# Modulation slots of the attentions, placed behind the value products of their step

## The chip, the cores and the metric

The kernel runs on one core of a Trainium2 chip. The metric is the time of one whole execution on the device, in microseconds (us). The five instruction queues of the core matter here by these names: PE is TensorE (PEld its weight loads, which overlap its products), DVE is VectorE, ACT is ScalarE, POOL is GpSimd, and SP is SyncE, which in this kernel only issues DMAs.

## What is computed

Two layers of a hybrid transformer step over 128 context tokens and 256 latent tokens, 384 tokens in three blocks of 128. Each layer modulates its input by vectors that come from a conditioning vector, mixes the tokens in three parallel branches, merges them by gates, and then runs a channel mixer (dense in layer 0, experts in layer 1). Cut to what matters:

```python
m = silu(cvec) @ w_ada[l] + b_ada[l]          # (1024,) @ (1024, 6144): the modulation
sh1, sc1, g1, sh2, sc2, g2 = split(m, 6)
h = rmsnorm(x, g) * (1 + sc1) + sh1
# mixer A, 4 heads, two maps each
p = softmax(q @ k.T * DHA ** -0.5)
oA = (p[map 0] - lam * p[map 1]) @ v          # then rmsnorm over the head
# mixer C, 8 heads on 2 key heads, a window of +-128 and a sink
oC = softmax(concat(scores, sink))[..., :-1] @ v
x = x + g1 * (sum_n sigmoid(h @ w_gate[n]) * (o[n] @ w_branch[n])) @ w_out
x = x + g2 * channel_mixer(rmsnorm(x, g') * (1 + sc2) + sh2)
```

## The kernel before

Everything is written out by hand: each engine has its own program, and semaphores are the only link between them. What stands earlier in an engine's program runs earlier on it.

**Large products.** A weight arrives in float32 in one of three buffers `raw` (slot number modulo 3). ACT copies it to `whi` (line 1571, or in two halves at line 1581), DVE computes `wlo = raw - whi` (line 2068), and PE multiplies in three passes (lines 779 to 781). SP issues the load of a slot only when the slot that had the buffer before it has been read.

**Modulation slots.** `w_ada` is not split. A slot of it is 1024 x 256 and is multiplied straight from `raw` by `ada_product` (line 796): eight products on four 32-column parts of the array, eight rows of the matrix at a time. Each slot lies in the same ring of three buffers as the other weights, and `mm_done` after it is what SP waits for before it fills that buffer again (line 522). Slots have no reader in the attention itself; their sums stay in bank 7 of PSUM and are copied out by ACT after the last of them.

**Attentions.** There are four: mixer A (kind 0) and mixer C (kind 1) in layer 0 and the same in layer 1. I call them the first to the fourth. Each has twelve steps t, a step being one head (A) or a pair of heads (C) with one block of queries; at t = 0, 3, 6, 9 the query block is that of the context and reads one block of keys, at the others it reads three. The parts of a step are:

- `scores(t)` on PE (line 1019): two products on the two halves of the array's rows, into banks 2(t%2) and 2(t%2)+1. It waits until the exponentials of t-2 have read those banks.
- `maxima(t)` on DVE (line 2250), then `exps(t)` on ACT (line 1744), then `normal(t)` on DVE (lines 2258 to 2265), which gives the weights in `ebuf`. DVE's program has `maxima(t+1)` ahead of `normal(t)`. In mixer C, DVE also adds half of a merge, `merge_sum` (line 2305), between `normal(4)` and `maxima(6)`.
- `transposes(t)` on PE (line 1037), the turn: it waits for `normal(t)`. In mixer C both maps are turned into banks 4 and 5 at every step, so it also waits for ACT's copy of the turn before it.
- `pt_copy(t)` on ACT (line 1755) takes the turned weights out of PSUM.
- `values(t)` on PE (line 1053), the value products: it waits for `pt_copy(t)`. `exps(t+2)` waits for `transposes(t)`, whose buffer it overwrites.

Ahead of the loop, scores 0 to 3 are done, and two modulation slots. In the loop PE runs, for each t: `scores(t+2)`, a modulation slot if t is in `ADA_STEPS` of this attention, `transposes(t)`, `values(t-1)`. `ADA_STEPS` is (1, 3, 5, 7, 9, 10), (1, 4, 6, 8, 10), (1, 4, 6, 9) and (1, 4, 6, 9) for the four attentions, 19 slots together. Right behind the loop PE goes on with the gate products of the next branch (lines 1110 and 1111).

Of the kernel before, what the change touches and what calls it, by code (L numbers as in the profile page):

```python
# [79 lines left out]
ADA_STEPS = {2: (1, 3, 5, 7, 9, 10), 3: (1, 4, 6, 8, 10), 4: (1, 4, 6, 9), 5: (1, 4, 6, 9)}  # L80
# [59 lines left out]
def prefix_step_kernel(nc, a, outs, const):  # L140
    y_prompt, y_sample, new_dk, new_dv, new_wk, new_wv = outs
    ctx = ExitStack()
    with ctx:
# [259 lines left out]
        def ada_slot(phase, i):  # L403

            if phase == 0:
                return FIRST_ADA[i]
            if phase == 1:
                return ADA_SLOTS[0] + 3 + RING * i
            l, kind = (phase - 2) // 2, (phase - 2) % 2
            return gate_slot(l, kind + 1, 0, 0) - ADA_SLOTS[phase] + i  # L410
# [17 lines left out]
        def ada_raw(n):  # L428

            return early[:, EARLY_BUF[n], :] if n in EARLY_BUF else raw[:, n % RING, :]  # L430
# [43 lines left out]
        def weight_col(t):  # L474

            return 1 + (T - P if t % 3 == 0 and t else 0)
# [24 lines left out]
        def raw_wait(eng, n, more=0):  # L501
            if n in EARLY_BUF:
                eng.wait_ge(side_in[EARLY_BUF[n]], early_wait(n))
            else:
                eng.wait_ge(raw_in[n % RING], more + 32 * raw_turn(n))
# [270 lines left out]
        def _(pe):  # L776
# [10 lines left out]
            def ada_product(phase, i):  # L787

                n, last, bank = ada_slot(phase, i), ADA_SLOTS[phase] - 1, 7
                if phase == 0:  # L790
                    i, last = i % 2, 1
                raw_wait(pe, n)
                w = ada_raw(n).rearrange("p (k c) -> p k c", k=KD)
                for k in range(KD):
                    j = k % 4
                    mm = pe.matmul(ps[32 * j:32 * j + 32, bank, 0:256], sil32[:, k, 30 - 2 * i:62 - 2 * i], w[:, k, :],  # L796
                                   start=(i == 0 and k < 4), stop=(i == last and k >= 4), tile_position=(0, 32 * j))
                mm.then_inc(mm_done, 1)
# [17 lines left out]
            def ada_end(phase, g=0):  # L816
                n = 2 * (GAP_SLOTS[phase] if phase in GAP_SLOTS else ADA_SLOTS[phase]) if phase else 4
                pe.wait_ge(ada_row, ada_turn(phase) if phase else g + 1)
                for c in range(2):
                    mm = pe.matmul(ps[:, 7, 256 + 32 * c:256 + 32 * c + n], adarow[:, c * P:(c + 1) * P], pick[:, 0:n],  # L820
                                   start=True, stop=True)
                mm.then_inc(ada_turned, 1)
# [185 lines left out]
            def scores(l, kind, t):  # L1008

                h, qb = t // 3, t % 3  # L1010
                if t >= 2:
                    pe.wait_ge(e_done, 24 * l + 12 * kind + t - 1)
                nk, k0 = (P, 0) if qb == 0 else (T, P)
                q, kk = (qTA, kTA[:, h, k0:k0 + nk]) if kind == 0 else (qTC, kTC[:, h // 2, k0:k0 + nk])
                for m in range(2):
                    r = slice(64 * m, 64 * m + 64)
                    c0 = score_col(t) if kind else 0
                    out, lhs = ps[:, 2 * (t % 2) + m, c0:c0 + nk], q[r, h, qb * P:(qb + 1) * P]
                    mm = pe.matmul(out, lhs, kk[r], start=True, stop=True)  # L1019
                mm.then_inc(s_done, 1)  # L1020

            def attention(l, kind):

                st0 = 24 * l + 12 * kind
                it0 = 24 * l + 12 * kind
                phase = 2 + 2 * l + kind

                def transposes(t):
                    pe.wait_ge(p_done, st0 + t + 1)
                    if kind:  # L1030
                        pe.wait_ge(pt_evac, it0 + t)
                    elif it0 + t >= 2:
                        pe.wait_ge(pt_evac, it0 + max(t - 1, 0))
                    k0 = kind * weight_col(t)
                    for m in range(1 + kind):
                        for kb in range(1 if t % 3 == 0 else 3):
                            mm = pe.transpose(ps[:, 4 + (m if kind else t % 2), kb * P:(kb + 1) * P],  # L1037
                                              ebuf[:, t % 2, m, k0 + kb * P:k0 + (kb + 1) * P], ident)
                    mm.then_inc(tp_done, 1)

                def values(t):
                    h, qb = t // 3, t % 3
                    pe.wait_ge(pt_evac, it0 + t + 1)
                    grp = 8 * l + 4 * kind + h
                    if qb == 0 and grp >= 1:
                        pe.wait_ge(o_evac, grp)
                    c = slice(h * P, (h + 1) * P) if kind == 0 else slice(512 + (h // 2) * 64, 576 + (h // 2) * 64)
                    keys = [vtok[:, 0, c]] if qb == 0 else [vtok[:, 1, c], vtok[:, 2, c], ctxv[:, c]]
                    for kb, v in enumerate(keys):
                        k = slice(kb * P, (kb + 1) * P)  # L1050
                        for m in range(1 + kind):
                            rows, x = (slice(64 * m, 64 * m + 64), ptm[:, t % 2, m, k]) if kind else (slice(0, P), pt[:, t % 2, k])
                            mm = pe.matmul(ps[rows, 6, qb * P:(qb + 1) * P], v, x, start=(kb == 0),  # L1053
                                           stop=(kb == len(keys) - 1))
                    mm.then_inc(pv_done, 1)

                scores(l, kind, 2)
                scores(l, kind, 3)
                pe.wait_ge(merge_top, 2 * l + kind + 1)
                ada_product(phase, 0)  # L1060
                ada_product(phase, 1)
                if kind == 0:
                    pe.wait_ge(merge_done, 6 * l + 2)
                else:
                    pe.wait_ge(merge_read, 4 * l + 2)
                for t in range(12):
                    if t >= 2 and t + 2 < 12:
                        scores(l, kind, t + 2)
                    if t in ADA_STEPS[phase]:
                        ada_product(phase, 2 + ADA_STEPS[phase].index(t))  # L1070
                    transposes(t)
                    if t >= 1:
                        values(t - 1)
                    if t == 11 and kind == 1:
                        ada_end(phase)
                values(11)
# [463 lines left out]
            for l in range(DEPTH):  # L1540
                if l:
                    mean_squares(2 * l)
                input_projection(l)
                branch(l, 0)
                attention(l, 0)
                branch(l, 1)
                attention(l, 1)
                branch(l, 2)
                out_projection(l)
                if l == 0:  # L1550
                    mean_squares(1)
                    units()
                else:
                    router()
                    experts()
# [1247 lines left out]
```

## Time and profile before

| | us |
|---|---|
| median of three runs | 1479.57 |
| lowest and highest of them | 1478.41, 1483.42 |
| the profiled execution | 1476.79 |
| its span in the profile | 1475.1 |
| PE busy | 1443.6 (98% of the span) |
| DVE busy | 906.6 |
| ACT busy | 729.5 |
| DMA, mean over the span | 221 GB/s |

PE is busy nearly all the time, and the granted clock is near full everywhere. The chain that ended last is PE's own work for 92% of the span. The four attentions take 25.7, 31.0, 24.7 and 30.2 us of the span. A matmul's duration in the profile overlaps the next one's, so what a piece of work costs PE is read from one start to the next start (I call this its pitch), and a wait of PE is the part of such a distance that the pitch doesn't explain.

### The profile page before, as it was taken

The numbers are of one execution on the slowest core, as the hardware profiler recorded it, in microseconds if no ns is written. First come the engines' busy times: TensorE is split into PE (matmuls) and PEld (weight loads), VectorE is DVE, ScalarE is ACT, GpSimd is POOL, SyncE is SP. The second block draws the span as 40 slices with busy tenths as digits, with TensorE's granted clock in tenths as the row PEclk, the third lists the DMA queues.
The fourth block names the chain that finished last, engine by engine and source line by source line (L and its number), as shares of the span: only waits on it lengthen the run. The fifth ranks groups of instructions, "written<-read, shape, count | busy, mean of one in ns | idle before, by whom it ended". The sixth has DMA issues, their size and how long they took to land.

```text
span 1475.1 us, 22230 instructions
## 1 busy us (share of the span) xinstructions
PE 1443.6 (98%) x8917; PEld 1273.5 (86%) x8917; DVE 906.6 (61%) x1092; ACT 729.5 (49%) x865; POOL 50.7 (3%) x55
## 2 busy tenths in 40 slices
PE   7999999999999999999999999999999999999997
PEld 5788969789999999998889879699888888888884
DVE  5543266555644345426532373747889999989888
ACT  4433354453433233225434272734568787787754
POOL 0100000000000000001000000000000000000020
PEclk9999999999999999999999999999999999999999
DMA  9854365468763355273532272655799999999991
GB/s 327 287 177 151 114 209 181 131 204 274 234 200 111 115 143 142 89 240 118 173 126 94 89 236 77 200 172 165 246 355 378 379 391 390 386 385 385 354 332 68
DMA packets 228858, 325.42 MB, mean 221 GB/s; under 512 B 8453, under 2 KB 154790, under 8 KB 228510
## 3 DMA queue, kind: packets, MB, share of 16 engines
q1 hardware_dynamic: 220160, 296.02, 59.0%
q0 software_dynamic: 6544, 24.83, 4.9%
q10 hardware_dynamic: 2062, 3.24, 0.6%
q8 instruction: 71, 1.16, 0.3%
q14 instruction: 21, 0.17, 0.0%
HBM read 309.09 MB, written 14.96 MB: 220 GB/s over the span
## 4 chain that ended last, share of the span: by engine, by line
PE 92%; DVE 3%; SPq 2%; DMA 1%; ACT 1%; issue 1%; DVEq 0%; ACTq 0%
PE ps L779 26%; PE ps L781 26%; PE ps L780 26%; PE ps L796 2%; PE ps L1019 2%; PE ps L1053 1%; SPq L522 1%; PE ps L1037 1%; PE ps L1301 1%; PE ps L1341 1%; DMA early<-in_w_ada_dram 1%; PE ps L874 1%; PE ps L998 0%; DMA raw<-in_w_ada_dram 0%; PE ps L806 0%
## 5 line engine op out<-in xcount | busy, mean ns | idle before, releaser
L779 PE MATMUL ps<-hhi,whi 128*128 128x384 f32 x824 | 276.7, 336 | 0.3 <-DVE hidlo L2688 0.3
L781 PE MATMUL ps<-hhi,wlo 128*128 128x384 f32 x824 | 275.5, 334 | 0.0
L780 PE MATMUL ps<-hlo,whi 128*128 128x384 f32 x824 | 275.4, 334 | 0.0
L2068 DVE TENSOR_TENSOR wlo<-raw,whi 128x2048 fp32r<-128x2048 f32 x65 | 148.7, 2289 | 173.8 <-ACT whi L1571 161.8
L779 PEld LDWEIGHTS ps<-hhi,whi 128*128 128x128 f32 x824 | 154.7, 188 | 2.4 <-issue 2.0
L780 PEld LDWEIGHTS ps<-hlo,whi 128*128 128x128 f32 x824 | 154.7, 188 | 0.3
L781 PEld LDWEIGHTS ps<-hhi,wlo 128*128 128x128 f32 x824 | 154.7, 188 | 0.0
L2560 DVE TENSOR_TENSOR wlo<-mraw,whi 128x2048 fp32r<-128x2048 f32 (+2 forms) x72 | 143.5, 1993 | 15.7 <-ACT whi L1841 15.1
L2560 DVE TENSOR_TENSOR wlo<-raw,whi 128x2048 fp32r<-128x2048 f32 (+2 forms) x72 | 144.2, 2019 | 10.1 <-ACT whi L1841 9.8
L1841 ACT ACTIVATE whi<-mraw 128x2048 fp32r<-128x2048 f32 (+2 forms) x72 | 120.9, 1679 | 58.0 <-PE ps L781 58.0
L1571 ACT ACTIVATE whi<-raw 128x2048 fp32r<-128x2048 f32 x60 | 114.6, 1912 | 70.6 <-PE ps L781 57.2
L779 PE MATMUL ps<-whi,xgh 128*128 128x512 f32 (+1 forms) x384 | 146.1, 380 | 1.0 <-DVE fin L2424 1.0
L781 PE MATMUL ps<-whi,xgl 128*128 128x512 f32 (+1 forms) x384 | 142.8, 372 | 0.0
L780 PE MATMUL ps<-wlo,xgh 128*128 128x512 f32 (+1 forms) x384 | 142.8, 372 | 0.0
L1841 ACT ACTIVATE whi<-raw 128x2048 fp32r<-128x2048 f32 (+2 forms) x72 | 121.6, 1698 | 35.8 <-PE ps L781 33.4
L779 PE MATMUL ps<-whi,hhi 128*128 128x512 f32 (+1 forms) x285 | 108.8, 382 | 2.9 <-issue 2.0
L2674 DVE TENSOR_TENSOR wlo<-raw,whi 128x2048 fp32r<-128x2048 f32 (+1 forms) x35 | 73.8, 2108 | 57.8 <-ACT whi L1818 57.8
L781 PE MATMUL ps<-whi,hlo 128*128 128x512 f32 (+1 forms) x285 | 106.1, 372 | 0.0
L780 PE MATMUL ps<-wlo,hhi 128*128 128x512 f32 (+1 forms) x285 | 106.0, 372 | 0.0
L1818 ACT ACTIVATE whi<-raw 128x2048 fp32r<-128x2048 f32 (+1 forms) x36 | 63.7, 1770 | 54.4 <-PE ps L781 54.4
L779 PEld LDWEIGHTS ps<-whi,xgh 128*128 128x128 f32 x384 | 72.2, 188 | 12.7 <-issue 3.1
L781 PEld LDWEIGHTS ps<-whi,xgl 128*128 128x128 f32 x384 | 72.1, 188 | 10.2
(413 smaller groups left out, 2483.9 us busy)
## 6 DMA issues: line engine op xcount, KB each, us to landing
raw<-in_w_ada_dram SPq DMA_DIRECT2D x62, 512.0 KB, 5.7
raw<-in_w_gate_dram SPq DMA_DIRECT2D x48, 512.0 KB, 4.6
raw<-in_w_ex_up_dram SPq DMA_DIRECT2D x24, 1024.0 KB, 8.2
raw<-in_w_ex_down_dram SPq DMA_DIRECT2D x24, 1024.0 KB, 6.8
raw<-in_w_in_dram SPq DMA_DIRECT2D x43, 512.0 KB, 6.1
raw<-in_w_ex_gate_dram SPq DMA_DIRECT2D x16, 1024.0 KB, 7.2
mraw<-in_w_ex_gate_dram SPq DMA_DIRECT2D x16, 1024.0 KB, 8.1
mraw<-in_w_ex_down_dram SPq DMA_DIRECT2D x16, 1024.0 KB, 8.4
```

The source lines that it names most:

```text
L522: sp.dma_start(dst[i], src[i]).then_inc(side_in[EARLY_BUF[n]] if n in EARLY_BUF else raw_in[n % RING], 16)
L779: pe.matmul(out, s[0], m[0], start=first, stop=False, **kw)
L780: pe.matmul(out, s[0], m[1], start=False, stop=False, **kw)
L781: return pe.matmul(out, s[1], m[0], start=False, stop=last, **kw)
L796: mm = pe.matmul(ps[32 * j:32 * j + 32, bank, 0:256], sil32[:, k, 30 - 2 * i:62 - 2 * i], w[:, k, :], start=(i == 0 and k < 4), stop=(i == ...
L1019: mm = pe.matmul(out, lhs, kk[r], start=True, stop=True)
L1571: act.activation(whi[:, n % RING, :], raw[:, n % RING, :], copy).then_inc(hi_done, 1)
L1818: act.activation(whi[:, s % RING, 0:used], raw[:, s % RING, 0:used], copy).then_inc(hi_done, 1)
L1841: act.activation(whi[:, m % RING, c:E_USED[m]], mraw[m % MRAW][:, c:E_USED[m]], copy).then_inc(hi_done, 1)
L2068: dve.tensor_tensor(wlo[:, n % RING, :], raw[:, n % RING, :], whi[:, n % RING, :].bitcast(F32), ALU.subtract).then_inc(lo_done, 1)
L2560: dve.tensor_tensor(wlo[:, m % RING, c:E_USED[m]], mraw[m % MRAW][:, c:E_USED[m]], whi[:, m % RING, c:E_USED[m]].bitcast(F32), ALU.subtrac ...
L2674: dve.tensor_tensor(wlo[:, s % RING, 0:used], raw[:, s % RING, 0:used], whi[:, s % RING, 0:used].bitcast(F32), ALU.subtract).then_inc(lo_d ...
```

## The change

In the loop of `attention` in PE's program the call of `ada_product` stands behind `values(t - 1)`; it stood ahead of `transposes(t)`. The slots, their steps and their order among themselves are the same, and the programs of the other four engines are word for word the same. No wait is added or removed.

```diff
                 for t in range(12):
                     if t >= 2 and t + 2 < 12:
                         scores(l, kind, t + 2)
-                    if t in ADA_STEPS[phase]:
-                        ada_product(phase, 2 + ADA_STEPS[phase].index(t))
                     transposes(t)
                     if t >= 1:
                         values(t - 1)
+                    if t in ADA_STEPS[phase]:
+                        ada_product(phase, 2 + ADA_STEPS[phase].index(t))
                     if t == 11 and kind == 1:
                         ada_end(phase)
                 values(11)
```

PE in the first attention, from scores 9 (the step t = 7) to turn 8, before. L1019 are scores, L796 is a modulation slot, L1037 a turn, L1053 value products.

```order
L1019 MATMUL ps<-kTA,qTA 128x128 x2
L796 MATMUL ps<-raw,sil_69 32x256 x8
L1037 MATMUL ps<-cst,ebuf 128x128 x3
L1053 MATMUL ps<-pt,vtok 128x128
L1019 MATMUL ps<-kTA,qTA 128x384 x2
L1037 MATMUL ps<-cst,ebuf 128x128 x3
```

The same place in the changed kernel:

```order
L1019 MATMUL ps<-kTA,qTA 128x128 x2
L1037 MATMUL ps<-cst,ebuf 128x128 x3
L1053 MATMUL ps<-pt,vtok 128x128
L796 MATMUL ps<-raw,sil_69 32x256 x8
L1019 MATMUL ps<-kTA,qTA 128x384 x2
L1037 MATMUL ps<-cst,ebuf 128x128 x3
```

The slot has moved from ahead of turn 7 to ahead of scores 10, so it now lies ahead of turn 8 and no longer ahead of turn 7.

PE in the second attention (mixer C, where a turn of three key blocks is six transposes), from scores 6 (the step t = 4) to turn 5, before:

```order
L1019 MATMUL ps<-kTC,qTC 128x128 x2
L796 MATMUL ps<-raw,sil_69 32x256 x8
L1037 MATMUL ps<-cst,ebuf 128x128 x6
L1053 MATMUL ps<-ptm,vtok 64x128 x2
L1019 MATMUL ps<-kTC,qTC 128x384 x2
L1037 MATMUL ps<-cst,ebuf 128x128 x6
```

and in the changed kernel:

```order
L1019 MATMUL ps<-kTC,qTC 128x128 x2
L1037 MATMUL ps<-cst,ebuf 128x128 x6
L1053 MATMUL ps<-ptm,vtok 64x128 x2
L796 MATMUL ps<-raw,sil_69 32x256 x8
L1019 MATMUL ps<-kTC,qTC 128x384 x2
L1037 MATMUL ps<-cst,ebuf 128x128 x6
```

Here the slot has moved from ahead of turn 4 to ahead of scores 7 and turn 5.

## Rows read from the trace of the kernel before

**Rows 1.** The profile page: PE busy, and the chain that ended last, by engine.
```profile
PE 1443.6 (98%) x8917; PEld 1273.5 (86%) x8917; DVE 906.6 (61%) x1092; ACT 729.5 (49%) x865; POOL 50.7 (3%) x55
...
PE 92%; DVE 3%; SPq 2%; DMA 1%; ACT 1%; issue 1%; DVEq 0%; ACTq 0%
```

**Rows 2.** Busy time by stretch: length, then each engine, clock, DMA share, GB/s.
```profile
194.94:220.68 25.74, 25.22 (x247) 15.59 (x245) 18.51 (x45) 16.84 (x54) 0.00 (x0) 1.00 0.91 293
276.37:307.39 31.02, 29.50 (x319) 17.78 (x317) 20.84 (x49) 21.00 (x58) 0.00 (x0) 1.00 0.74 239
841.77:866.45 24.68, 23.50 (x215) 14.77 (x213) 18.51 (x45) 16.97 (x54) 0.00 (x0) 1.00 0.78 256
922.16:952.33 30.17, 28.57 (x303) 17.35 (x301) 21.03 (x50) 21.43 (x58) 0.00 (x0) 1.00 0.64 210
...
866.45:922.16 55.71, 55.71 (x351) 52.57 (x350) 27.19 (x22) 21.99 (x30) 0.00 (x0) 1.00 0.35 114
```

**Rows 3.** Timeline of PE, start of the first attention: start, us, what.
```profile
194.94 1.93 PE L796 MATMUL ps<-raw,sil 128*32 128x256 f32 x32
...
196.80 0.33 PE L1037 MATMUL ps<-cst,ebuf 128*128 128x128 f32 x1
...
197.06 1.07 PE L796 MATMUL ps<-raw,sil 128*32 128x256 f32 x16
```

**Rows 4.** Timeline of PE and DVE, first attention, step t = 7.
```profile
209.63 0.49 PE L1019 MATMUL ps<-kTA,qTA 64*128 64x128 f32 x4
210.05 1.07 PE L796 MATMUL ps<-raw,sil 128*32 128x256 f32 x16
210.13 0.62 DVE L2261 SCALAR_TENSOR_TENSOR ebuf<-ebuf,small 128x384 f32<-128x384 f32 x1
211.05 0.55 PE L1037 MATMUL ps<-cst,ebuf 128*128 128x128 f32 x3
211.75 0.92 PE L1019 MATMUL ps<-kTA,qTA 64*128 64x384 f32 x4
212.60 0.55 PE L1037 MATMUL ps<-cst,ebuf 128*128 128x128 f32 x3
```

**Rows 5.** Timeline of DVE, ACT and PE, end of the first attention.
```profile
217.86 0.62 DVE L2261 SCALAR_TENSOR_TENSOR ebuf<-ebuf,small 128x384 f32<-128x384 f32 x1
218.50 1.05 ACT L1581 ACTIVATE whi<-raw 128x1024 fp32r<-128x1024 f32 x1
218.53 0.55 PE L1037 MATMUL ps<-cst,ebuf 128*128 128x128 f32 x3 [0.23 <-DVE ebuf L2261]
219.99 0.71 PE L1053 MATMUL ps<-pt,vtok 128*128 128x128 f32 x4 [0.24 <-ACT pt L1755]
```

**Rows 6.** Timeline of PE and ACT, second attention, step t = 1.
```profile
278.60 1.07 PE L796 MATMUL ps<-raw,sil 128*32 128x256 f32 x16
278.71 0.38 ACT L1755 ACTIVATE ptm<-ps 128x256 f32<-128x256 f32 x1 [5.03 <-PE ps L1037]
```

**Rows 7.** Timeline of PE and DVE, second attention, steps t = 4 and 5.
```profile
285.68 1.07 PE L796 MATMUL ps<-raw,sil 128*32 128x256 f32 x16
286.07 0.42 DVE L2265 TENSOR_SCALAR ebuf<-ebuf,small 128x384 f32<-128x384 f32 x1
286.40 1.75 DVE L2305 TENSOR_TENSOR macc<-macc,gbuf 128x1536 f32<-128x1536 f32 x1
289.40 0.88 PE L1037 MATMUL ps<-cst,ebuf 128*128 128x128 f32 x6 [0.63 <-DVE ebuf L2265]
```

**Rows 8.** Timeline of PE, second attention, steps t = 10 and 11.
```profile
301.30 1.07 PE L796 MATMUL ps<-raw,sil 128*32 128x256 f32 x16
...
302.59 0.87 PE L1037 MATMUL ps<-cst,ebuf 128*128 128x128 f32 x6 [0.21 <-DVE ebuf L2265]
...
304.45 0.85 PE L1037 MATMUL ps<-cst,ebuf 128*128 128x128 f32 x6 [0.54 <-ACT ptm L1755]
```

**Rows 9.** SP's DMA issues behind the first attention's slots 5 and 6.
```profile
211.18 5.55 SPq L522 DMA_DIRECT2D raw<-in_w_gate_dram  x4
```

## Prediction

> **What bounds the kernel now.** I read four views, in this order. The page says that PE is busy for 98% of the span and that the chain which ended last runs over PE for 92% of it [rows 1]. The stretches of the four attentions come next: 25.74, 31.02, 24.68 and 30.17 us, 111.61 us together, all at the full granted clock, with DVE and ACT busy for 18 to 22 us of each [rows 2]. PE is the bound there too, but with small gaps, and DVE and ACT lag closely behind it. Then the stretch between the third and fourth attention: PE is busy for all of its 55.71 us [rows 2]. So what an attention loses or gains is carried to the end one for one. Last, the timelines of the attentions, to see what each turn and each value product waited for. The question is how much of PE's waiting the slots cover where they stand, and how much they would cover one place later.
>
> **What the change moves.** PE does the same work; 19 of its pieces change place. Two things can alter the time: the cost of switching from one kind of product to another, and the waits.
>
> *Switches.* A slot followed by a turn has a pitch of 1.00 (210.05 to 211.05) [rows 4]. The two slots at the start, one behind the other, take 1.86 together, so a slot followed by a slot costs 0.86 [rows 3]: leaving the slot's four column parts costs 0.14. Scores cost the same 0.84 to 0.85 ahead of a turn (211.75 to 212.60 [rows 4]) as ahead of a slot, and value products cost the same ahead of scores and ahead of a slot. Per step with scores, the old row is values, scores, slot, turn and the new one values, slot, scores, turn: three switches each. The one kind of step in the new row that no trace shows is slot to scores, at 14 places (t up to 8 in the four attentions). I take 1.00 as for slot to turn, the nearest row; its bounds are 0.86 (no cost of leaving) and 1.14 (twice that cost).
> The Trainium skill, in "TensorEngine Tiling (Array Packing)", section Key Properties, says that changing the tiling mode drains TensorE. By that rule too both rows pay for three changes per step, so the sum would be the same; the 0.14 behind the slots agrees with a drain, and no row here shows the one from column parts straight to row halves.
> In the two mixer A attentions one gain is certain: turn 0 ahead of a slot has a pitch of 0.26 (196.80 to 197.06) [rows 3] against 0.16 ahead of other work, so 0.10 goes in each.
>
> *Waits that come.* The operand of a turn is there 0.67 after the start of the last operation of `normal` in mixer A (217.86 to 218.53, where the turn waited) [rows 5], and 0.47 after it in mixer C. At a slot's step the turn will be asked for one slot earlier than now, when the scores end. In the first attention at t = 7 the scores end at 210.05, and the operand is there at 210.13 + 0.67 = 210.80 [rows 4]: PE, which hid this under a slot of 1.00, waits 0.75. At t = 3, 5 and 9 the operand is there by then, give or take 0.08. In the second attention at t = 4 the scores end at 285.68 and the operand is there at 286.07 + 0.47 = 286.54: a wait of 0.86 [rows 7]. At t = 10 the value products end at 301.30, the operand comes at 302.59: a wait of 1.29, of which 0.29 is there already [rows 8]. At t = 1, turn 1 must also wait for the copy of turn 0, which starts at 278.71, takes 0.38 and is seen 0.07 later, at 279.16; PE could turn at 278.60, so it waits 0.56 [rows 6].
>
> *Waits that go.* The slot now stands between value products and the next scores, so the turn of the next step comes 1.00 later after its own chain began. In the second attention turn 5 waited 0.71 for a `normal` that stood behind the merge's 1.75 [rows 7]; with the slot of t = 4 ahead of it, it won't. Turn 11 waited about 0.6 [rows 8]; with the slot of t = 10 behind turn 10 it won't. In the first attention turn 11 waited 0.30 and value product 11 0.36 [rows 5]; the slot of t = 10 covers both.
>
> *Sum.* These cannot simply be added, because an earlier turn lets ACT and DVE run earlier, and a later one later. So I laid out each attention's steps on PE, ACT and DVE anew, each piece starting when its engine is free and its last operand has arrived, with the pitches and delays of the rows. In the old order this gives 25.84, 30.98, 24.56 and 30.15 us, 111.53 together against the trace's 111.61 [rows 2]. PE's waits in the old and the new order are then:
> First attention: old 0.85 (turns 2, 8, 11, value product 11). New 1.50: turn 7 0.77, and six waits of 0.06 to 0.19 (value products 0, 6 and 9, turns 2, 5 and 10). With the 0.10 of the pitch: +0.54.
> Second: old 1.79 (turn 5 0.71, scores 10 0.17, turn 10 0.29, turn 11 0.62). New 2.72 (turn 1 0.56, turn 4 0.87, turn 10 1.29): +0.93.
> Third: old 1.58 (0.98 of it turn 11). New 2.17 (turn 4 0.77, turn 11 0.68, and five small ones): +0.51 with the pitch and rounding.
> Fourth: old 1.96 (turns 5, 8, 10, 11 and two small ones). New 2.34 (turn 1 0.56, turn 4 0.87, turn 10 0.29, turn 11 0.62): +0.38.
> Together +2.36. In the trace the third attention holds about 0.1 more than the layout, for a slot that waited for its DMA; the new order is later than that load. I take +2.3 us. With slot to scores at 0.86 the same layout gives +1.0, with 1.14 it gives +4.2.
>
> *Buffers freed later.* A slot's end is what SP waits for. In the first attention slots 5 to 7 end 1.7 to 1.9 us later. Behind slot 5, SP issues the first gate weights at 211.18 [rows 9]; their first half took about 5 us to land, and ACT reads them at 218.50 [rows 5]. Moved by 1.7 they land at about 218.3, and ACT would ask at 218.6. The copy of turn 11 stands behind that read on ACT, but has 0.45 to spare. I price this at nothing; if the cover goes, it is up to 1 us, in that attention. The others have no slot so near the end or fewer slots, and their loads more room.
>
> On the profiled execution of 1476.79 this gives 1479.1. The median of the runs, 1479.57, lies 2.8 above that execution, so as a median I expect 1479.57 + 2.3 = 1481.9.
>
> **Rivals.**
> (a) *The cover goes nowhere.* The pipeline of scores, exponentials and turns follows PE's pace so closely that each wait that comes is paid back at the next turn, and the sum is 0 within 0.5: 1479.6. For it: in the second attention turns 4 and 5 do just that (0.87 comes, 0.71 goes). Against it: turn 7 in the first attention comes with no partner, since turn 8's old wait was under 0.1 [rows 4].
> (b) *Faster.* The earlier turns free `ebuf` and start the copies earlier, so that DVE gets ahead and the new waits stay away, while the old ones at turns 5 and 11 go. All waits that vanish in my layout are worth 3.8 us, with the 0.3 of the DMA wait 4.1: 1475.5. For it: `exps(t+2)` waits for turn t by the program. Against it: in both cases above DVE's `normal` is held by `maxima` and the merge, which follow scores, and scores don't come earlier.
> (c) *Slower by more than the bound.* Slot to scores costs 1.14 at all 14 places, since the scores' weights go to row halves while the column parts still drain (+4.2), and the gate weights of the first attention land behind the read (+1): +5.2, 1484.8. It decides from a pitch of about 1.14 on. For it: the DMA share of that stretch is 0.91 [rows 2]. Against it: a slot's end cost 0.14 ahead of a turn.
> (d) *The change does nothing on the chip*, because PE reaches the slots early anyway. The order on PE excludes it: a slot whose turn is not ready now stands behind that turn.
>
> **How the numbers follow.** About 0.3% (4.4 us) is what a measurement can tell from no change. Forecast, +1.0 to +4.2: 0.62. (a): 0.16. (b), any gain beyond 0.5: 0.09, of which a third passes the bound. (c): 0.13. So faster 0.03, same 0.84, slower 0.13. The range must hold the forecast's own (1480.6 to 1483.8), (a) and most of (b) and (c), and the scatter of the three runs (1478.4 to 1483.4): 1476.5 to 1486.
>
> **What would show it.** The stretch from the first slot to the first gate product should measure 26.3, 31.9, 25.1 and 30.5 us. Turn 7 of the first attention should wait 0.77 for DVE with the slot behind it, turn 4 of the second 0.87, turn 10 of the second 1.29, turn 1 of the second 0.56 for ACT; turns 5 and 11 of the second should not wait. A slot ahead of scores should have a pitch of 1.00. The stretches between the attentions should keep their lengths. The prediction is wrong if the pitch of slot to scores is far from 1.00, if those turns don't wait, or if a gate product behind an attention waits for weights.

## The result, and the profile after

The changed kernel takes 1481.18 us (median of 20 runs, 1479.24 to 1483.68), the kernel before 1478.22 (20 runs, 1476.20 to 1483.42). The ratio is 1.0018, with a 95% interval from 1.0011 to 1.0025: 1.6 to 3.7 us more, slower than before by more than nothing and by less than the 0.3% that the prediction took as its bound. Forecast were +2.3 us and a median of 1481.9.

The stretches that answer to those of [rows 2], from the first modulation slot to the first gate product of each attention, then the stretch between the third and the fourth, and the rest behind the fourth (columns as there):

```profile
195.03:221.55 26.52, 25.66 (x246) 15.60 (x245) 18.32 (x45) 17.22 (x54) 0.00 (x0) 1.00 0.83 272
277.26:309.26 32.00, 29.42 (x319) 17.76 (x317) 20.84 (x49) 21.10 (x58) 0.00 (x0) 1.00 0.64 212
843.64:868.64 25.00, 23.72 (x214) 14.76 (x213) 18.31 (x45) 17.22 (x54) 0.00 (x0) 1.00 0.74 234
924.35:954.94 30.59, 28.46 (x302) 17.34 (x300) 21.03 (x50) 21.53 (x58) 0.00 (x0) 1.00 0.62 207
868.64:924.35 55.71, 55.71 (x352) 52.57 (x350) 27.19 (x22) 21.98 (x30) 0.00 (x0) 1.00 0.37 123
954.94:1479.40 524.46, 511.61 (x2927) 440.73 (x2925) 442.62 (x442) 342.52 (x286) 36.92 (x28) 0.99 0.86 310
```

The attentions take 114.11 us together against 111.61: 0.78, 0.98, 0.32 and 0.42 more, +2.50. The stretch between the third and the fourth has kept its 55.71 to the hundredth, so what an attention loses is indeed carried on. DVE's and ACT's busy times in the attentions moved by less than 0.4. The two profiled executions differ by 4.3 us in their spans; the 1.7 that the attentions don't explain lie in the last stretch, in the router, and go with the granted clock there (at the end of the next part). In the attentions the granted clock is 1.00 before and after, so it has no part in the +2.50.

The timeline of PE in the first attention around the step t = 7, with DVE's operation that makes turn 7's operand, against [rows 4]:

```profile
209.70 0.49 PE L1019 MATMUL ps<-kTA,qTA 64*128 64x128 f32 x4
210.21 0.62 DVE L2261 SCALAR_TENSOR_TENSOR ebuf<-ebuf,small 128x384 f32<-128x384 f32 x1
210.88 0.55 PE L1037 MATMUL ps<-cst,ebuf 128*128 128x128 f32 x3 [0.69 <-DVE ebuf L2261]
211.44 0.46 PE L1053 MATMUL ps<-pt,vtok 128*128 128x128 f32 x2
211.83 1.07 PE L796 MATMUL ps<-raw,sil 128*32 128x256 f32 x16
212.83 0.92 PE L1019 MATMUL ps<-kTA,qTA 64*128 64x384 f32 x4
```

Scores 9 end at 209.70 + 0.42 = 210.12, and the turn starts at 210.88: it waits 0.76 for `normal` of step 7, and the slot that covered this stands behind the value products. (The bracket of a row, 0.69 here, counts the idle time from the end that the profile gives the piece ahead, which lies behind the end by pitch, and so is smaller.) The slot followed by scores has a pitch of 1.00 (211.83 to 212.83), the one kind of step that no row of before showed.

The turns of the second attention that wait, and two that don't any more (turn 5 at 291.05, turn 11 at 306.29), on PE:

```profile
280.12 0.85 PE L1037 MATMUL ps<-cst,ebuf 128*128 128x128 f32 x6 [0.56 <-ACT ptm L1755]
...
288.03 0.88 PE L1037 MATMUL ps<-cst,ebuf 128*128 128x128 f32 x6 [0.79 <-DVE ebuf L2265]
...
291.05 0.88 PE L1037 MATMUL ps<-cst,ebuf 128*128 128x128 f32 x6
...
304.04 0.87 PE L1037 MATMUL ps<-cst,ebuf 128*128 128x128 f32 x6 [1.21 <-DVE ebuf L2265]
...
306.29 0.88 PE L1037 MATMUL ps<-cst,ebuf 128*128 128x128 f32 x6
```

These are turns 1, 4, 5, 10 and 11. What turns 5 and 11 waited before [rows 7, 8] is gone; what turns 1, 4 and 10 wait instead is more.

### The profile page after: what moved, and what is told of

The parts are those of the page before. It is cut to its first block, busy times and chain, and to the rows that moved or that the text cites. A ratio compares the mean times of both kernels' runs of the same rounds, so it can differ in the third digit from the quotient of the medians.

```text
span 1479.4 us, 22230 instructions
## 1 busy us (share of the span) xinstructions
PE 1445.6 (98%) x8917; PEld 1274.9 (86%) x8917; DVE 906.0 (61%) x1092; ACT 730.1 (49%) x865; POOL 50.8 (3%) x55
## 3 DMA queue, kind: packets, MB, share of 16 engines
q8 instruction: 71, 1.16, 0.3%
## 4 chain that ended last, share of the span: by engine, by line
PE 93%; DVE 3%; SPq 2%; DMA 1%; issue 1%; ACT 0%; DVEq 0%
PE ps L779 26%; PE ps L780 26%; PE ps L781 26%; PE ps L796 2%; PE ps L1019 2%; PE ps L1053 2%; PE ps L1037 2%; SPq L522 1%; PE ps L1301 1%; PE ps L1341 1%; DMA early<-in_w_ada_dram 1%; PE ps L874 1%; DVE small L2250 1%; PE ps L998 0%; PE ps L806 0%
## 5 line engine op out<-in xcount | busy, mean ns | idle before, releaser
L2250 DVE TENSOR_REDUCE small<-ps 128x2 f32<-128x768 f32 (+3 forms) x48 | 37.0, 778 | 72.5 <-PE ps L1019 71.7
```

The source lines that it names most:

```text
L2250: dve.tensor_reduce(small[:, p, 0:2], ps[:, 2 * p:2 * p + 2, c], X, ALU.max, negate=True).then_inc(nmax_done, 1)
```

## The experiments

The theory is that the loss of the attentions lies in cover alone: a turn's operand comes at a time that PE's order hardly moves, and a slot of 1.00 ahead of that turn hides the wait for it, while a slot behind the value products covers the turn of the next step. Rivals are the later release of the ring's buffers, a cost of each move in itself (a switch of the array), and waits that simply add up. For each experiment I give the four attentions from its trace (stable to 0.01 or 0.02 us from kernel to kernel where nothing in them was changed and no DMA was waited for), and the ratio of the whole to the kernel before. By "the layout" I mean the same laying out of the steps on PE, ACT and DVE as in the prediction.

**Late release alone.** PE's order is that of before. SP also waits for the value products of the step.

```diff
                     sp.wait_ge(mm_done, prior + 1)
+                    for p, ts in ADA_STEPS.items():
+                        if prior - ada_slot(p, 2) in range(len(ts)):
+                            sp.wait_ge(pv_done, 12 * (p - 2) + ts[prior - ada_slot(p, 2)])
```

> PE's order is that of before; only SP waits longer with the load that follows a moved slot, until the value products of the slot's step are done, so the buffers come free as late as in the changed kernel. Cover theory (the loss comes from turns that the slots no longer cover): the four attentions keep 25.7, 31.0, 24.7 and 30.2 us and the whole differs by under 1 us. Late-release rival (the loss comes from the ring's loads landing later): the four attentions or the stretches behind them are longer, by the 2.5 us that the changed kernel's attentions gained.

The four attentions took 25.73, 31.02, 24.67 and 30.17 us, as before to 0.01. The whole had a ratio of 1.0010 (1.0000 to 1.0019); with 0 to 2.8 us this alone doesn't exclude the rival, but the stretches do: those between the attentions have kept their lengths too (55.71, 534.35 and 55.68). The rest goes with the granted clock: the runs at a mean clock of 0.997 took 1478.59 on average (5 runs) and 1478.46 in the kernel before (14 runs).

This edit delays the loads by less than the change does. Behind slot 5 of the first attention, SP issues the first gate weights at 211.18 before, at 211.93 here and at 212.96 in the changed kernel. What settles the rival is the changed kernel's own trace. PE waits there for no load of a slot's or a gate's weights in or behind the attentions, and the first gate product behind the first attention starts 0.14 after the last value product's start, as before (221.41 to 221.55, and 220.54 to 220.68). Buffers freed later cost nothing there.

**Cover kept.** Ten slots moved, nine left ahead of their turn.

```diff
+ADA_BEHIND = {2: (3, 5, 9, 10), 3: (6, 8), 4: (6, 9), 5: (6, 9)}
...
-                    if t in ADA_STEPS[phase]:
+                    if t in ADA_STEPS[phase] and not (t in ADA_BEHIND[phase]):
                         ada_product(phase, 2 + ADA_STEPS[phase].index(t))
                     transposes(t)
                     if t >= 1:
                         values(t - 1)
+                    if t in ADA_STEPS[phase] and t in ADA_BEHIND[phase]:
+                        ada_product(phase, 2 + ADA_STEPS[phase].index(t))
```

> As the changed kernel, but the slots at t = 1 and 7 of the first attention, 1, 4 and 10 of the second, 1 and 4 of the third and fourth stay ahead of their turn. Cover theory, by the layout of the rows of before: the attentions change against before by -0.3, -0.2, -0.3 and -0.3 us, -1.1 together; no wait at turn 7 of the first, and at turns 1 and 4 of the second. A rival by which moving a slot costs something in itself, at each place: 10 of 19 slots moved, so about half of the 2.5 us that the changed kernel's attentions lost, +1.3.

The attentions took 25.48, 30.83, 23.98 and 29.83 us: -0.26, -0.19, -0.70 and -0.34, -1.5 together (0.28 of it in the third, whose slot no longer waited for its load). The whole: 0.9994 (0.9984 to 1.0004). The layout, which has no cost for the move itself, gives -1.1, or -1.4 with that load; a cost at each move would give +1.3. Nothing is left for a cost of moving in itself.

**Cover lost.** The other nine moved, the ten left: the same code with `ADA_BEHIND` as (1, 7), (1, 4, 10), (1, 4) and (1, 4).

> The complement of the run before it: only the slots at t = 1 and 7 of the first attention, 1, 4 and 10 of the second, 1 and 4 of the third and fourth stand behind the value products. Cover theory, by the layout: +0.8, +1.1, +0.7 and +0.7 us in the four attentions, +3.3 together, more than the whole change cost. A cost in itself of each moved slot: 9 of 19, +1.2.

The four stretches:

```profile
195.44:222.21 26.77, 25.57 (x246) 15.60 (x245) 18.52 (x45) 16.81 (x54) 0.00 (x0) 1.00 0.87 278
277.92:310.13 32.21, 29.50 (x319) 17.75 (x317) 20.95 (x49) 21.02 (x58) 0.00 (x0) 1.00 0.65 211
844.52:869.95 25.43, 23.77 (x214) 14.78 (x213) 18.52 (x45) 16.94 (x54) 0.00 (x0) 1.00 0.77 248
925.64:956.56 30.92, 28.60 (x302) 17.32 (x301) 21.13 (x50) 21.34 (x58) 0.00 (x0) 1.00 0.63 205
```

They are 1.03, 1.19, 0.75 and 0.75 longer, +3.7, more than with all 19 moved, and the whole has a ratio of 1.0032 (1.0020 to 1.0045). Nine slots carry the whole loss; the other ten give 1.5 us back, and the two parts add up to 2.2 against 2.5 for the change.

**In the middle.** All slots between the turn and the value products.

```diff
-                    if t in ADA_STEPS[phase]:
-                        ada_product(phase, 2 + ADA_STEPS[phase].index(t))
                     transposes(t)
+                    if t in ADA_STEPS[phase]:
+                        ada_product(phase, 2 + ADA_STEPS[phase].index(t))
                     if t >= 1:
                         values(t - 1)
```

> All slots stand between the turn and the value products of their step. Cover theory, by the layout: the turn loses its cover as in the changed kernel and the value products gain one: +0.4, +1.3, +0.4 and +0.7 us in the four attentions, +2.8 together, with turn 7 of the first waiting 0.77, turns 1, 4 and 10 of the second 0.56, 0.87 and 1.29. If it is the place between value products and scores that costs, this kernel stays at 0.

The attentions took 26.67, 32.26, 25.44 and 30.92 us: +0.93, +1.24, +0.76 and +0.75, and the whole 1.0033 (1.0022 to 1.0045). So it isn't the place ahead of the scores that costs. In mixer C this is the layout to 0.06. In mixer A it is 0.5 and 0.4 more than the layout. PE's timeline in the first attention, from turn 5, shows a part of the reason:

```profile
205.88 0.55 PE L1037 MATMUL ps<-cst,ebuf 128*128 128x128 f32 x3
206.35 1.07 PE L796 MATMUL ps<-raw,sil 128*32 128x256 f32 x16
207.36 0.71 PE L1053 MATMUL ps<-pt,vtok 128*128 128x128 f32 x4
```

A turn ahead of a slot has a pitch of 0.47, ahead of value products 0.38. The value products behind the slot cost more too: their first four products take 0.54 (207.36 to 207.90), against 0.45 directly behind a turn (207.09 to 207.54 before). That is 0.18 at a place where the turn and its value products stood together before. Both use the whole array in mixer A, so a slot between them adds a switch of the array that the other two places don't have. In mixer C the value products use 64 columns, the turn is followed by a switch in any case, and its pitch is 0.80 or 0.81 ahead of either (288.06 to 288.86 here, 288.03 to 288.84 in the changed kernel). How these costs and the waits add up to just 0.5 and 0.4 was not laid out.

**The merge sum one step later, old order.** PE's order is that of before.

```diff
-                    if t == 5 and kind:
+                    if t == 6 and kind:
                         merge_sum(l)
```

> PE's order is that of before; in the two mixer C attentions DVE does the merge sum of 1.75 us one step later, behind normal 5 and no longer behind normal 4. Cover theory, by the layout: turn 5, which waited 0.71 for normal 5, does not wait any more, so the second and fourth attention change by -0.7 each, -1.4 together, the first and third by 0.

The second and fourth attention took 30.31 and 29.46 us, -0.71 each, and turn 5 follows scores 7 without a wait (0.85 after 287.91):

```profile
287.91 0.92 PE L1019 MATMUL ps<-kTC,qTC 64*128 64x384 f32 x4
288.76 0.87 PE L1037 MATMUL ps<-cst,ebuf 128*128 128x128 f32 x6
```

The first took 25.95 instead of 25.74, with nothing changed in it: the slot at t = 5 started 0.21 late for its load. The third took 24.40 instead of 24.68, its slot not having waited. Slots ahead of their turn are that close to their loads. The whole: 0.9991 (0.9982 to 1.0000).

**The merge sum one step later, new order.** The same edit in the changed kernel.

> The same step of the merge sum in the changed kernel. Cover theory, by the layout: there the slot behind the value products of t = 4 covers turn 5 already, and turns 1, 4 and 10 wait as before, so nothing is gained: the four attentions take 26.5, 32.0, 25.0 and 30.6 us as in the changed kernel, against before +0.8, +1.0, +0.3 and +0.4. If waits simply add up, it gains 1.4 against the changed kernel.

The attentions took 26.51, 32.01, 25.00 and 30.59 us, as in the changed kernel to 0.01, and the whole 1.0013 (1.0004 to 1.0022). The same 1.75 us of DVE's work is worth 0.71 where a turn waits behind it and nothing where a slot covers that turn. Waits don't add up.

**DVE's order at turn 7, in both orders of PE.** What sets the time of a turn's operand? In the first attention alone, `normal(7)` ahead of `maxima(8)`:

```diff
-                    maxima(t)
-                    if t == 2:
-                        continue
-                    normal(t - 1)
+                    if phase == 2 and t == 8:
+                        normal(7)
+                        maxima(8)
+                    else:
+                        maxima(t)
+                        if t == 2:
+                            continue
+                        normal(t - 1)
```

In the changed kernel:

> The changed kernel, but in the first attention DVE does normal 7 ahead of maxima 8. The claim: turn 7 waits because its operand is made behind maxima 8, which follows scores 8, so an earlier turn cannot be had by asking earlier. If that holds, the layout gives no wait at turn 7 and a first attention of 25.6 us, 0.8 below the layout of the changed kernel (26.4; measured 26.5). If normal 7 is late for ACT's exponentials instead, turn 7 waits 0.7 as before and the attention stays at 26.5.

In the kernel before:

> The same swap of normal 7 and maxima 8 on DVE, with PE's order of before. There the slot covers turn 7, so an earlier operand brings nothing, and maxima 8 comes later, which delays exponentials 8, scores 10 (a wait of 0.46) and turn 8 (0.28): the layout gives a first attention of 26.4 to 26.5 us, 0.7 more than the 25.74 of before. If an earlier operand is a gain wherever it is made, it takes less than 25.7.

The first attention took 25.76 us in the changed kernel, 0.76 less than with the change alone, and turn 7 follows the end of scores 9 at once (0.42 after 209.52):

```profile
209.52 0.49 PE L1019 MATMUL ps<-kTA,qTA 64*128 64x128 f32 x4
209.94 0.55 PE L1037 MATMUL ps<-cst,ebuf 128*128 128x128 f32 x3
```

In the kernel before it took 26.44 us, 0.70 more, as laid out. Scores 10 wait there for the exponentials of step 8 and turn 8 for its operand. By pitch these waits are 0.31 and 0.27, where the layout had 0.46 and 0.28:

```profile
212.07 0.92 PE L1019 MATMUL ps<-kTA,qTA 64*128 64x384 f32 x4 [0.25 <-ACT ebuf L1744]
213.18 0.55 PE L1037 MATMUL ps<-cst,ebuf 128*128 128x128 f32 x3 [0.19 <-DVE ebuf L2261]
```

So the wait at turn 7 comes from DVE's order: its operand is made behind the maxima of scores that PE itself has just done. That order is the better one with the slot ahead of the turn and the worse one with the slot behind it. Each of the two kernels ran once (1480.08 and 1478.78 us, beside 1478.51 for the kernel before), so this rests on the stretch and not on the whole.

**A faster version.** Slots where the layout has them cover the longest waits, and the merge sum one step later.

```diff
-ADA_STEPS = {2: (1, 3, 5, 7, 9, 10), 3: (1, 4, 6, 8, 10), 4: (1, 4, 6, 9), 5: (1, 4, 6, 9)}
+ADA_STEPS = {2: ((1, 3, 5, 7, 9), (10,)), 3: ((1, 6), (3, 9, 10)), 4: ((1, 4, 6), (9,)), 5: ((1, 4, 6, 9), ())}
...
+                next_slot = list(range(2, ADA_SLOTS[phase]))
...
-                    if t in ADA_STEPS[phase]:
-                        ada_product(phase, 2 + ADA_STEPS[phase].index(t))
+                    if t in ADA_STEPS[phase][0]:
+                        ada_product(phase, next_slot.pop(0))
                     transposes(t)
                     if t >= 1:
                         values(t - 1)
+                    if t in ADA_STEPS[phase][1]:
+                        ada_product(phase, next_slot.pop(0))
```

> Slots placed where the layout has them cover the longest waits: first attention ahead of the turn at t = 1, 3, 5, 7, 9 and behind the value products at 10; second ahead at 1 and 6, behind at 3, 9 and 10; third ahead at 1, 4, 6 and behind at 9; fourth all ahead; the merge sum behind normal 5. By the layout: -0.35, -1.2, -0.3 and -0.7 us, -2.5 together against before, so a ratio of about 0.998. If the remaining waits just move to other turns, 0.

```profile
195.19:220.80 25.61, 25.36 (x246) 15.59 (x245) 18.52 (x45) 16.95 (x54) 0.00 (x0) 1.00 0.92 291
276.51:306.37 29.86, 29.47 (x318) 17.74 (x316) 20.86 (x49) 21.08 (x58) 0.00 (x0) 1.00 0.69 222
840.72:864.75 24.03, 23.43 (x214) 14.76 (x213) 18.36 (x45) 17.14 (x54) 0.00 (x0) 1.00 0.74 241
920.46:949.92 29.46, 28.56 (x303) 17.34 (x301) 21.05 (x50) 21.41 (x58) 0.00 (x0) 1.00 0.67 215
```

The attentions change by -0.13, -1.16, -0.65 and -0.71, -2.65 together, and the whole takes 1475.29 us at a ratio of 0.9983 (0.9974 to 0.9992). It is faster than the kernel before by 1.2 to 3.8 us, and so than the changed one. Of the 2.65, 1.42 is the later merge sum alone (the run in the old order); the places of the slots, and loads that weren't waited for, give the rest. In the second attention PE is busy for all but 0.4 us.

**The last stretch.** The 1.7 us of the two profiled executions that the attentions don't explain are in neither theory. The granted clock in the 10 us around the router's wait, as stretches of the kernel before, of the changed kernel, and of the old order with the merge sum later:

```profile
1080.00:1090.00 10.00, 8.71 (x51) 8.27 (x52) 6.53 (x9) 6.31 (x6) 0.88 (x1) 1.00 0.86 331
```
```profile
1080.00:1090.00 10.00, 7.87 (x40) 7.54 (x39) 5.06 (x7) 4.16 (x3) 1.17 (x1) 0.83 0.97 378
```
```profile
1080.00:1090.00 10.00, 10.00 (x44) 9.90 (x44) 4.12 (x4) 4.42 (x4) 0.48 (x1) 0.67 0.68 274
```

Before, the clock stayed at its upper level of 2.4 GHz; after, it was at 0.83 of it on average, and in the third kernel at 0.67, being at its lower level of 1.2 GHz for a part of the stretch. PE had waited 2.1 us for the router's choice shortly before, in every kernel of this document. In the changed kernel the granted clock was 0.50 in both us from 1085 to 1087, while PE was busy all the time. A mean of 0.83 over 10 us is 1.7 us of full clock lost, which is what this stretch took more; in the third kernel 0.67 makes 3.3 of the 4.2 that it took more. From the end of the fourth attention to PE's last product, the kernels whose clock stayed up took 513.4 (before) and 513.5 us (new order with the merge sum later), those with 0.83 to 0.88 here 515.0 to 515.2, and those with 0.66 and 0.67 516.5 and 517.6. PE's old order of slots stands in all three groups (before, the swap on DVE, and late release and the merge sum), so it isn't the change that chooses. The scatter of the whole goes with the clock as well: of the 27 runs of the kernel before that stand beside the later merge sum and the faster version, those with a mean clock of 0.998 took 1476.6 us on average, those with 0.997 1478.4 and those with 0.996 1480.0. Why the clock falls in some executions and not in others is left open.

## Why the prediction was right

*The bound.* PE's own work and the small waits in it set the attentions, and the rest follows one for one: the stretch between the third and the fourth kept its 55.71. Right. One reading is off: DVE and ACT are busy for 16.8 to 21.4 us of each attention [rows 2], not for 18 to 22; nothing was worked out from it.

*The switches.* Slot to scores has a pitch of 1.00, as taken from slot to turn, and not 0.86 or 1.14. The rule of the Trainium skill ("TensorEngine Tiling (Array Packing)", Key Properties), that a change of tiling mode drains TensorE, agrees as far as the change goes: the number of changes per step is the same before and after, and so is their cost. (It is three in mixer A. In mixer C, whose value products use 64 columns, it is four in both orders, where the prediction says three throughout.) No run here separates the drain's own price from that of work that no longer overlaps.

*The waits that come.* Turn 7 of the first attention was to wait 0.77 and waited 0.76. Turns 1, 4 and 10 of the second were to wait 0.56, 0.87 and 1.29. From the end of the piece before, by its pitch, to the turn's start it was 0.63 at turn 1 (279.12 + 0.37 to 280.12), 0.86 at turn 4 and 1.29 at turn 10. *The waits that go* went, at turns 5 and 11.

*The sum.* Laid out were 26.38, 31.91, 25.07 and 30.53 us; measured are 26.52, 32.00, 25.00 and 30.59. The sum of the differences to before was +2.36, or +2.3 with the load, and is +2.50. The largest miss is in the first attention, +0.78 for +0.54. The old order was laid out 0.10 too long there (25.84 for 25.74), and why is open; the new one was laid out 0.14 too short. The term that was too small in the new one is what a waited-for piece costs behind its wait: value product 6, which waited for the copy of its bank, has a pitch of 0.39 (211.44 to 211.83), against 0.32 for one that didn't wait. There are three such places in the new order (value products 0, 6 and 9) and one of that pitch in the old one (value product 3), so two more, about 0.17 together. The layout took the same pitch with and without a wait.

*The load.* The third attention was to lose its wait for a load with the slot later. It did: 25.00 in each of the three kernels with this attention in the new order (the changed kernel, the one with the later merge sum, the one with the swap), while in the old order it was 24.68, 24.67, 24.40 and 24.40, as the load came. The term was too small: the prediction took 0.1 for it, the distance between the trace and its layout (24.68 and 24.56), but in that trace the slot starts 0.28 late (scores at 849.48, a pitch of 0.42, the slot at 850.18), and without this wait the attention takes 24.40. So the layout of the old order was 0.16 too long, and the new order costs this attention 0.3 where the old one waits for the load and 0.6 where it doesn't, for a layout of 0.5.

*Buffers freed later* were priced at nothing, and the changed kernel's trace confirms it: no slot and no gate product of the attentions waits for its load.

*The rivals.* (a), that each wait is paid back at the next turn, holds only where a wait goes as another comes, as at turns 4 and 5 in mixer C, and the merge sum shows that pair from both sides. (b), that earlier turns let DVE get ahead, fails for the reason given: `normal` stands behind `maxima` on DVE, and only the swap of those two removes the wait. (c), a dearer switch with a late load, didn't occur.

*The median.* The forecast of 1481.9 started from 1479.57, the median of three runs; twenty give 1478.22. So the start was 1.35 too high. The change itself was +2.7 by the ratio (0.18%) and +3.0 between the two medians, for a forecast of +2.3. The two errors partly cancel, and that 1481.9 came so near to 1481.18 is in part luck.

## What to carry to other kernels

In a pipeline where one in-order engine alternates between pieces that wait and filler that doesn't, filler belongs ahead of the piece whose operand comes last, not behind it. Which piece that is can be read before the change: compare the end of the piece ahead with the arrival of the operand, turn by turn, and then lay out the whole chain once, since an earlier piece does not bring its operand earlier when the other engine makes it behind work that follows the same engine. A wait that is covered is worth nothing when it is shortened, so look where the filler stands before moving work on the other engines.

## What the hardware showed that was not expected

- In mixer A a slot between a turn and value products costs 0.18 us more than at a place where the array is switched anyhow: the turn's pitch is 0.47 for 0.38, and that of the first four value products 0.54 for 0.45. The prediction had a row of this kind for the turn: turn 0 with 0.26 ahead of a slot and 0.16 ahead of other work.
- A value product that had to wait has a pitch 0.07 us longer than one that didn't (0.39 against 0.32). In both cases the load of its first weights no longer overlaps the piece ahead: it starts 0.11 ahead of the product directly behind a turn (206.98 for 207.09, before), but 0.03 ahead where the product had waited (211.41 for 211.44, changed kernel) and 0.01 behind a slot (207.35 for 207.36, slots in the middle).
- The granted clock fell beside the same wait of 2.1 us in some executions and not in others, with up to 4 us between them in the last stretch, more than the change itself.
